# Second FFN, up projection, rounds 4 to 10: every unit as seven block products, with the weight sums made early in DRAM

## The reference, cut to what matters

```python
h = rms_norm_2(x, ffn_norm_g[l]) * (1 + scale_f) + shift_f
u, v = jnp.split(h @ w_up[l], 2, axis=-1)
u = causal_depthwise_conv(u, conv_w[l], conv_b[l])      # 3 taps along the tokens
x = x + gate_f * ((jax.nn.silu(u) * v) @ w_down[l])
```

## Time and profile before

| | us |
|---|---|
| median of 3 runs | 1345.59 (1345.52 to 1347.8) |
| the profiled execution | 1345.38 |
| its span, first to last instruction | 1343.4 |
| PE busy | 1331.0 |
| rounds 3 to 9, first block product to the first plain tile behind them (1043.77 to 1191.38) | 147.6 |

### The profile page before, as it was taken

The page is one execution under the profiler, slowest core; times in us unless marked ns, Lnnn a source line. Parts: engine busy times, 40 slices in busy tenths (PEclk is TensorE's granted clock), DMA queues, the critical chain, the costliest instruction groups (busy, mean ns, idle before and its releaser), DMA issues.

```text
span 1343.4 us, 21993 instructions
## 1 busy us (share of the span) xinstructions
PE 1331.0 (99%) x8268; PEld 1135.0 (84%) x8268; DVE 857.3 (64%) x1682; ACT 624.0 (46%) x1097; POOL 658.7 (49%) x369
## 2 busy tenths in 40 slices
PE   8999999999999999999999999999999999999998
PEld 7878888888998888888889976788998999988887
DVE  5898876456778676767897879724579454431222
ACT  7236566564364445453222525675344454542222
POOL 7555232126254444445553489733364776654441
PEclk9999999999999999999999999999999999999999
DMA  7931121115525444444673241121242223252221
GB/s 218 227 102 41 56 63 49 30 35 172 173 87 180 141 142 147 152 149 141 202 228 107 77 112 48 50 64 48 79 157 94 93 96 115 75 201 97 86 87 63
DMA packets 188903, 150.59 MB, mean 112 GB/s; under 512 B 21625, under 2 KB 186723, under 8 KB 188304
## 3 DMA queue, kind: packets, MB, share of 16 engines
q1 hardware_dynamic: 187104, 148.78, 35.8%
q10 hardware_dynamic: 1200, 0.36, 0.1%
q0 software_dynamic: 512, 0.25, 0.1%
HBM read 145.18 MB, written 4.19 MB: 111 GB/s over the span
## 4 chain that ended last, share of the span: by engine, by line
PE 93%; DVE 4%; ACT 1%; issue 1%; POOL 0%; DMA 0%; DVEq 0%; ACTq 0%
PE ps L2638 28%; PE ps L2639 27%; PE ps L2640 27%; PE ps L2832 2%; PE ps L2888 1%; PE ps L2917 1%; DVE qd L2291 1%; DVE hf L2299 1%; PE ps L3120 1%; PE ps L3164 0%; PE ps L3149 0%; PE ps L2722 0%; PE ps L3093 0%; PE ps L3186 0%; DVE hs L2334 0%
## 5 line engine op out<-in xcount | busy, mean ns | idle before, releaser
L914 POOL TENSOR_TENSOR w_lo<-raw,w_hi 128x1024 fp32r<-128x1024 f32 (+2 forms) x210 | 487.2, 2324 | 569.2 <-ACT w_hi L1021 436.0
L2638 PE MATMUL ps<-h_hi,w_hi 128*128 128x512 f32 (+1 forms) x1308 | 478.4, 366 | 0.1
L2639 PE MATMUL ps<-h_lo,w_hi 128*128 128x512 f32 (+1 forms) x1308 | 474.1, 362 | 0.0
L2640 PE MATMUL ps<-h_hi,w_lo 128*128 128x512 f32 (+1 forms) x1308 | 473.5, 362 | 0.0
L2638 PEld LDWEIGHTS ps<-h_hi,w_hi 128*128 128x128 f32 x1308 | 247.2, 189 | 41.9 <-issue 5.0
L2640 PEld LDWEIGHTS ps<-h_hi,w_lo 128*128 128x128 f32 x1308 | 247.1, 189 | 38.7
L1021 ACT ACTIVATE w_hi<-raw 128x1024 fp32r<-128x1024 f32 (+2 forms) x166 | 164.7, 995 | 244.4 <-PE ps L2640 222.9
L2639 PEld LDWEIGHTS ps<-h_lo,w_hi 128*128 128x128 f32 x1308 | 247.4, 189 | 35.6
L2638 PE MATMUL ps<-g_hi,w_hi 128*128 128x512 f32 (+1 forms) x394 | 144.9, 368 | 0.0
L2640 PE MATMUL ps<-g_hi,w_lo 128*128 128x512 f32 (+1 forms) x394 | 144.4, 366 | 0.0
L2639 PE MATMUL ps<-g_lo,w_hi 128*128 128x512 f32 (+1 forms) x394 | 144.3, 366 | 0.0
(11 more groups left out here) (408 smaller groups left out, 1999.2 us busy)
## 6 DMA issues: line engine op xcount, KB each, us to landing
ada<-in_ada_w SPq DMA_DIRECT2D x48, 512.0 KB, 3.7
raw<-in_ffn_w_up SPq DMA_DIRECT2D x22, 1024.0 KB, 4.9
raw<-in_w_up SPq DMA_DIRECT2D x22, 1024.0 KB, 4.9
raw<-in_w_in SPq DMA_DIRECT2D x21, 1024.0 KB, 5.1
raw<-in_ffn_w_down SPq DMA_DIRECT2D x8, 896.0 KB, 5.9
raw<-in_w_down SPq DMA_DIRECT2D x8, 896.0 KB, 5.0
raw<-in_w_in SPq DMA_DIRECT2D x16, 256.0 KB, 3.7
raw<-in_w_out SPq DMA_DIRECT2D x4, 1024.0 KB, 5.1
```

Source lines behind the costliest of these rows:

```text
L914: pool.tensor_tensor(w_lo[slot % 4][:, 0:nk, :], part[:, :, slot % 2 * P:(slot % 2 + 1) * P], w_hi[slot % 4][:, 0:nk, :].bitcast(F32), ALU ...
L2638: pe.matmul(out_ap, w, x, start=first, stop=False, **kw)
L2639: pe.matmul(out_ap, w, xl, start=False, stop=False, **kw)
L2640: return pe.matmul(out_ap, wl, x, start=False, stop=last, **kw)
```

## The change

What was done for u is done for v as well: rounds 3 to 9 consist of 14 pairs of tiles (`NPAIR`), each made of seven products, and no plain tile is left in them. The order of the products on PE is the list `PRODUCTS`: of pair p the products 6 and 2, the next pair's 1, then 7 and 3, the next pair's 5, then 4. Each product has half a weight buffer (`half_slot`), so that ACT may begin a product's high part when PE has ended the product eight places before. The pairs use PSUM banks 4 to 7 and 0 to 3 in turn.

The four sums of weight blocks are no longer made by DVE in each round. They are made once, for all seven rounds, in DRAM (`kept_sums`, four tensors of 2 x 512 x 7 x 128): POOL issues 8 DMAs that copy a block (`begin_sum`, one behind the low part of each of the tiles 20 to 27) and 8 DMAs that add another block or an earlier sum (`add_to_sum`, behind tiles 30, 31, 32, 33, 34, 36, 38, 40). A DMA moves 512 x 7 x 128 floats. The first 12 have pieces of 128 floats, the last four, which add one sum to another, pieces of 896. POOL waits for landings at three places: for the 8 copies ahead of the first addition, for the first four additions ahead of the fifth (behind tile 34), for six ahead of the seventh (behind tile 38). SP then loads, for each pair, three blocks early and the rest late (`early_blocks`, `late_blocks`): six DMAs in place of one, 1792 KB in place of 1024 KB.

The low parts are split between two engines: products 2, 3 and 4 have theirs made by DVE (`DVE_LOWS`), products 1, 5, 6 and 7 by POOL. The sums are formed with the other sign in part, so that the second tile of a pair comes out negative; its taps and the product with v are multiplied by -1 at no extra instruction but one on DVE ahead of the FFN. The space that DMA descriptors of POOL take in SBUF is halved (8192 bytes a partition), and the 8192 bytes hold the loaded sums (`sums`).

```diff
 R0, R1 = 3, FT // 2 - 1
-IN_ORDER = (1, 5, 6, 2, 7, 3, 4)
+PAIR_TILE, AFTER = S_UP2 + 4 * R0, S_UP2 + 4 * R1
+NPAIR = (AFTER - PAIR_TILE) // 2
+
+
+PRODUCTS = [(0, 1), (0, 5)]
+for _p in range(NPAIR):
+    PRODUCTS += [(_p, 6), (_p, 2)] + [(_p + 1, 1)] * (_p + 1 < NPAIR) + [(_p, 7), (_p, 3)] \
+        + [(_p + 1, 5)] * (_p + 1 < NPAIR) + [(_p, 4)]
+PRODUCT = {x: q for q, x in enumerate(PRODUCTS)}
+NQ = len(PRODUCTS)
+DVE_LOWS = (2, 3, 4)
...
+def product_lows(p, j):
+
+    mine = [x for x in PRODUCTS[:PRODUCT[p, j] + 1] if (x[1] in DVE_LOWS) == (j in DVE_LOWS)]
+    return len(mine) if j in DVE_LOWS else PAIR_TILE + len(mine)
+
+
+def w_slot(s):
+    return s % 4 if s < AFTER else (PAIR_TILE + NQ // 2 + s - AFTER) % 4
+
+
+def half_slot(p, j):
+    q = PRODUCT[p, j]
+    return (PAIR_TILE + q // 2) % 4, slice(q % 2 * 4, q % 2 * 4 + 4)
 
...
+        def early_blocks(p):
+
+            c = up_columns(R0 + p // 2, p % 2)
+            return [(w_of(p, 1), k_tiles(a["w_up_2"][0], 0, 4, c, P)), (w_of(p, 5), kept_sum(1, p)), (w_of(p, 6), kept_sum(2, p))]
+
+        def late_blocks(p):
+
+            c = up_columns(R0 + p // 2, p % 2)
+            view = raw[(PAIR_TILE // 2 + p) % 2][:, :].rearrange("p (k n) -> p k n", k=KD)
+            return [(view[:, 4:8, :], k_tiles(a["w_up_2"][0], 4 * P, 4, c)), (w_of(p, 7), kept_sum(3, p)), (w_of(p, 3), kept_sum(4, p))]
+
+        def kept_blocks(kind, t, kh):
+
+            c = up_columns(R0, kind)
+            w = a["w_up_2"][0][kh * 4 * P:(kh + 1) * 4 * P, c:c + (R1 - R0) * 256]
+            return w.rearrange("k (r t n) -> k r t n", t=2, n=P)[:, :, t, :]
```

SP, POOL (the line numbers in the changed kernel are 983 for `begin_sum`, 993 for `add_to_sum`):

```diff
+            sp.wait_ge(sums_kept, SUMS_BEGUN + 16 * 8)
+            sp.wait_ge(freed["dve"], FREED[up_tile(0, 1, 1)][1])
+            for p in range(NPAIR):
+                n = PAIR_TILE // 2 + p
+                if p < 2:
+                    after_lows(2 * n - 3)
+                else:
+                    sp.wait_ge(lo_done, product_lows(p - 2, 6))
+                for dst, src in LOADS[n]:
+                    sp.dma_start(dst, src).then_inc(raw_in[n % 2], 16)
+                if p >= 2:
+                    after_lows(2 * n - 3)
+                for dst, src in late_blocks(p):
+                    sp.dma_start(dst, src).then_inc(late_in[n % 2], 16)
+            for n in range(AFTER // 2, S_DOWN2 // 2 + 2):
                 unit(n)
...
+            def begin_sum(n, kind):
+
+                t, kh = {1: (1, 0), 2: (0, 0), 3: (0, 0), 4: (0, 1)}[n]
+                pool.dma_start(kept_sums[n - 1][kind], kept_blocks(kind, t, kh)).then_inc(sums_kept, 16)
+
+            def add_to_sum(n, kind):
+
+                if n == 1:
+                    pool.wait_ge(sums_kept, SUMS_BEGUN)
+                elif n in (2, 4):
+                    pool.wait_ge(sums_kept, SUMS_BEGUN + 16 * (4 if n == 2 else 6))
+                more = {1: lambda: kept_blocks(kind, 1, 1), 2: lambda: kept_sums[0][kind],
+                        3: lambda: kept_blocks(kind, 1, 0), 4: lambda: kept_sums[1][kind]}[n]()
+                pool.dma_start(kept_sums[n - 1][kind], more, accum_op=ALU.add, max_dma_last_dim=4 * (R1 - R0) * P).then_inc(sums_kept, 16)
+
+            SUM_STEPS = dict(zip(range(S_MERGE + 2, S_MERGE + 10), itertools.product((1, 2, 3, 4), range(2))))
+            ADD_STEPS = dict(zip([S_MERGE + 12, S_MERGE + 13, S_MERGE + 14, S_MERGE + 15] + [S_ATTN + 2 * n for n in range(4)],
+                                 itertools.product((1, 3, 2, 4), range(2))))
 
             def tables():
```

ACT and DVE (in the changed kernel 2535 is `product_low`, 2607 `seed_c12`, 2611 `make_c22`):

```diff
+            def product_hi(q):
+
+                if q >= NQ:
+                    return
+                p, j = PRODUCTS[q]
+                u = PAIR_TILE // 2 + p
+                if q < 8:
+                    act.wait_ge(tile_done, PAIR_TILE - 3 + q // 2)
...
                     act.wait_ge(raw_in[u % 2], RAW_COUNT[u])
                 else:
-                    act.wait_ge(w_summed, ONCE + 4 * (r - R0) + {5: 1, 7: 2, 6: 3, 3: 4}[j])
-                act.activation(w_hi[w][:, ks, :], w_of(r, j), ACT.Copy).then_inc(hi_done, 1)
+                    act.wait_ge(late_in[u % 2], LANDED + 48 * (p // 2 + 1))
...
+            for p in range(NPAIR):
+                r, kind = R0 + p // 2, p % 2
+                last = R0 + (p - 1) // 2
+                q0 = PRODUCT[p, 6] + 7
+                if p and not kind:
+                    g_high(last, 0)
+                if kind:
+                    first_tap(last, 1)
+                if p == NPAIR - 1:
+                    hi(AFTER)
+                product_hi(q0)
+                if kind:
+                    silu(last, 0)
+                product_hi(q0 + 1)
+                if p == NPAIR - 1:
+                    hi(AFTER + 1)
+                if kind:
+                    silu(last, 1)
+                elif p:
+                    g_high(last, 1)
+                product_hi(q0 + 2)
+                if p + 1 < NPAIR:
+                    copy_one(p + 1)
+                    product_hi(q0 + 3)
...
+                if p + 1 < NPAIR:
+                    product_hi(q0 + 5)
+                    copy_five(p + 1)
+                    product_hi(q0 + 6)
+            hi(AFTER + 2)
...
+            def product_low(p, j):
+                w, ks = half_slot(p, j)
+                dve.wait_ge(hi_done, product_splits(p, j))
+                dve.tensor_tensor(w_lo[w][:, ks, :], w_of(p, j), w_hi[w][:, ks, :].bitcast(F32), ALU.subtract).then_inc(low_by_dve, 1)
+
...
+            for p in range(NPAIR):
+                r, kind = R0 + p // 2, p % 2
+                last = R0 + (p - 1) // 2
+                if kind:
+                    taps2(last, 1)
+                elif p:
+                    gated_up(last, 1)
+                product_low(p, 4)
+                seed_c12(p)
+                if p + 1 < NPAIR:
+                    product_low(p + 1, 2)
+                if p and not kind:
+                    g_low(last, 0)
+                if not kind:
+                    g_low(last, 1)
+                make_c22(p)
+                if p + 1 < NPAIR:
+                    product_low(p + 1, 3)
+                if kind:
+                    gated_up(r, 0)
+                else:
+                    taps2(r, 0)
```

PE:

```diff
-                pe.wait_ge(lo_done, SPLIT_NO[r, j])
+                if j in DVE_LOWS:
+                    pe.wait_ge(low_by_dve, ONCE + product_lows(p, j))
+                else:
+                    pe.wait_ge(lo_done, product_lows(p, j))
                 if j == 1:
-                    pe.wait_ge(freed["dve"], FREED[up_tile(r - 1, 0, 0)][1])
+                    pe.wait_ge(freed["dve"], FREED[PAIR_TILE + 2 * (p - 2) if p > 1 else PAIR_TILE - 4][1])
...
                 elif j == 7:
-                    pe.wait_ge(c12_seeded, ONCE + r - R0 + 1)
+                    pe.wait_ge(c12_seeded, ONCE + p + 1)
                 elif j == 4:
-                    pe.wait_ge(c22_made, ONCE + r - R0 + 1)
+                    pe.wait_ge(c22_made, ONCE + p + 1)
...
-            for r in range(R0, R1):
-                s = up_tile(r, 1, 0)
-                product(r, 1)
...
+            for p, j in PRODUCTS:
+                product(p, j)
+            pe.wait_ge(freed["dve"], after_pair(NPAIR - 2))
+            for s in range(AFTER, S_DOWN2):
                 tile(s, h_hi, h_lo)
```

349 lines of the change are left out of this document (150 added, 199 removed).

## The result

The changed kernel took 1375.2 us in the median of four runs (1370.9 to 1376.7), the kernel before 1346.7 beside it: ratio 1.020, 95% interval 1.017 to 1.024. Forecast were 1339.7 us. The profiled execution took 1376.2 us (span 1374.1), 30.8 more than that of before.

The account below looks back on a forecast made before the run. PE was taken as the bound. From the profiled 1345.38 us, 5.9 came off in the block rounds and all else cost 0: 1339.5, with the median 0.2 above, 1339.7; 8 in 10 range 1338 to 1355.

Parts of the forecast that it names:

- PE's gain: Block rounds 3 to 9: seven rounds of matmuls fall from 147.0 to 141.1 us, 5.9 us gained; stage forecast 141.7.
- Engines beside PE: Block rounds, per pair of 10.08 us: ACT 7.3, POOL 5.6, DVE 6.5 to 9.5; none becomes the bound.
- The tightest hand-off: Pairs of v in the block rounds: product 7 waits for `seed_c12`, ready at 4.0 us, wanted by PE at 4.3.
- It just fits: Pairs of v: the seed is ready before PE wants it, with 0.1 to 0.3 us to spare.
- DVE ends at 3.6: Pairs of v: DVE's low part, begun at 2.5 beside POOL's, ends 3.6 us after product 4 of the pair before.
- The rival of a late seed: Block rounds: seed at 4.9, PE stands 0.5 to 0.8 us a pair, 4 to 9 us, 1345 in all; chance 0.15.
- POOL's time for a DMA: Merge gates: issuing a DMA of 3584 pieces holds POOL 2 to 3 us; up to 6.6 us costs nothing.
- Landing of an addition: Sums in DRAM, from 218.5 us: an addition takes 16 us to land, between 10 and 30.
- Cost 0: Sums in DRAM: additions land before tiles 35 and 39 need POOL's low parts, so they cost nothing, with thin cover.
- Additions land late: Rival: POOL waits for landings behind tiles 34 and 38, about 20 us slower, 1360; decides from 17.6 us; chance 0.20.
- Loads: Block rounds: 1792 KB a pair at DMA share 0.6 to 0.7, hidden; DRAM sums: eight DMAs fit beside the loads.
- Slow descriptors: Rival: POOL needs 15.9 us to issue each DMA in the merge gates, about 1420 us in all; chance 0.10.

Follow-up runs that it names:

- with the seed in time, the one without additions, low part first: Changed kernel without its eight additions, DVE's low part of product 4 put ahead of the taps in each pair: 1343.4 us, ratio 0.9963.
- the last kernel above: Changed kernel with product 4's low part first, copies behind tiles 21 to 24 and 34 to 37, additions behind 27, 29, 31, 33, 144, 146, 148, 149: 1343.3 us.
- the spread kernel with copies from tile 18: Changed kernel with copies behind tiles 18 to 25, additions behind 27, 29, 31, 33, 144, 146, 148, 149, product 4's low part first: 1350.6 us.

## Why the prediction was wrong, step by step

**PE's gain: right.** 5.9 us were forecast; with the seed in time the rounds took 141.40 us against a forecast of 141.7, 6.2 less than before. In the changed kernel they took 143.8, a gain of 3.8; the 2.4 missing are the one wait in the last pair.

**Engines beside PE: right, somewhat high.** In the rounds DVE was busy 84.9 / 14 = 6.1 us a pair (forecast 6.5 to 9.5), ACT 6.5 (7.3), POOL 5.7 (5.6), the DMA share 0.55 (0.6 to 0.7).

**The tightest hand-off: right for 13 pairs, missed in the last.** "It just fits" held where I counted, a middle pair. I had not counted the edge, where POOL's operation is a plain low part of 128x1024 (2.41 us, back to back with a second) and not one of 128x512. What did not hold there is "DVE ends at 3.6" beside POOL's low part: here DVE's took 2.47 us, 1.8 more than the 0.68 it takes alone, and ended 0.5 us behind the first of POOL's two (1214.24 + 2.4 is 1216.6; DVE ended at 1217.2). The rival of a late seed is thus true in one pair of 14.

**POOL's time for a DMA: right.** A copy of 3584 pieces held POOL 2.2 to 2.4 us (2 to 3 taken), an addition 3.6 (1.0 where it reads sums), all under the 6.6 that were free. But that limit spoke only of PE's lead over POOL in the merge gates. It did not speak of what stands behind the issue for another engine, such as low parts of the queries. Nor did it speak of DVE: while POOL issues a DMA, and again while it makes a low part, `sc` of DVE stands. With a copy alone beside it, issued at 283.61 for 2.34 us in the last kernel above, two multiplications took 2.62 us in place of 1.00:

```profile
284.04 2.62 DVE L2087 TENSOR_SCALAR sc<-sc,stat,gates 128x512 f32<-128x512 f32 x2
```

I had that hold in the block rounds, between two low parts, and put it at nothing in the merge gates, where DVE is what PE waits for in the 1.3 us of the changed kernel and in most of the 9 with the copies two tiles earlier.

**Landing of an addition: the size right, the overlap wrong. This is the step that failed.** I took 16 us; the median of all eight is 16.7 (12.9 to 20.2), and the four that read `w_up_2` took 16.4 to 18.8. "With 16 us, overlapping in part, this holds" took two in flight at once. Up to the seventh none were: POOL stood until the one before had landed, 65 us in all. The first four took from 220.84 to 292.38, 17.9 us each against my own limit of 17.6 from 218.5. The fifth and the sixth followed one after the other and landed at 319.29, where I had them by 300. So "Cost 0" was 17.6 us at tile 39.

**Its rival: right in kind, too small.** "Additions land late" had 0.20 and 20 us, with POOL behind tiles 34 and 38 the place, and 17.6 us the point from which it decides. For what it counted it was near: 17.6 us by tile 39. At tile 35 nothing waited in the end: its low part was there by 296.3 us at the latest, and PE, late by then through its waits for DVE, began the tile at 305.04. The price was 29 us because the rival left out two things. An addition makes other loads late: 15.1 us for 512 KB in place of 3.3, which is 9.0 us more by the convolution branch. And PE that had stood was granted half its clock behind it, 2.4 us there. The runs with the additions in the first down projection show the late loads by themselves: POOL had time there, and the loss was larger, not smaller.

**Loads: right for copies, put at nothing for additions without a reason.** I had "Eight in 72 us fit beside the loads, which leave the engines mostly idle there", of copies. For additions there is no such sum; the rival names the loads of 512 KB, without a price. For copies that is right (0.3 us in the median). An addition holds the engines far longer for the same bytes. Worked out from the share of the software queue: in the spread kernel with copies from tile 18, 0.753 x 80 us / 4 = 15.1 us of all engines for an addition from `w_up_2`, 0.563 x 70 / 4 = 9.9 us for one from sum to sum, against 0.481 x 85 / 8 = 5.1 for a copy. The share adds up the times of packets and can pass 1.00 (1.01 and 1.06 above), so these are estimates of what an addition takes, and best read against one another.

```profile
q0 software_dynamic: 14390, 7.34, 75.3%
...
q0 software_dynamic: 2112, 7.34, 56.3%
...
q0 software_dynamic: 3712, 14.68, 48.1%
```

The three rows are the software queue's packets, MB and share from 195 to 275 and 870 to 940 us of that spread kernel and from 120 to 205 us of the one without additions, low part first. The Trainium skill, Collectives: The Full Stack, § The bandwidth ceiling, has an add at half the rate of a copy. From sum to sum that is what the trace shows (9.9 against 5.1); for the additions from `w_up_2` it is a third (15.1). There the rows hold 14390 packets for four additions, some 3600 each, where eight copies have 3712, 464 each. That the small packets are the reason is likely, and no run here separated it.

**Slow descriptors: did not come** (0.10).

The chances stood at 0.24 for slower. The forecast rested on a cover that I had called thin; the limit of 17.6 us against a landing taken as 16 with ends at 10 and 30 would have borne far more than 0.20 for that rival, and its own 1360 already lay outside the range of 8 in 10.

## What to carry to other kernels

Before a DMA is put on an engine's queue as "hidden", ask three things of its place: how long until the next one may be issued (the engine stands, with all that is queued behind), which loads land in the same stretch, and who else waits for what stands behind the issue or, like DVE here, stands itself while it is made. Spread to stretches with few loads, with the additions from `w_up_2` 20 us apart and nothing due behind a landing, sixteen such transfers cost 1.4 us here (1343.3 against 1341.9, intervals that overlap); bunched, they cost 30 (1375.2 against 1344.9).

For two engines that cannot run the same form side by side, count the hand-off at the edges of a stage too, where the neighbour's operation is another size, and put the one that PE waits for first.

## What the hardware showed that I had not expected

- An adding DMA from DRAM to DRAM held the DMA engines 15.1 us for 1.8 MB in 512-byte pieces and 9.9 in 3584-byte ones, a copy 5.1, by the times of its packets.
- While POOL issued a DMA of 3584 pieces, a DVE operation between SBUF operands stood: two of 128x512 took 2.62 us beside the issue of a copy (2.34 us), and 5.16 beside that of an addition with a low part queued behind it, in place of 1.00.
- With additions of 512-byte pieces the next DMA was not issued before the one before had landed; of copies the second was (125.64 and 132.99 us in the kernel without additions, 10.3 and 12.7 us to landing), and the third, the fifth and the seventh stood 5.2, 4.3 and 3.5 us, until the one before had landed. From sum to sum it went both ways: in the changed kernel the sixth addition stood 9.96 us until the fifth had landed, with no wait in the program for that, and the eighth did not stand; in the recurrence the last two, 9.9 us apart, did not either. The likeliest reason is room for descriptors in the queue of POOL; no run here changed it.
- Loads of 512 KB took 15.1 and 19.3 us to land beside an addition, 3.3 without; beside plain copies of the same bytes 4.8 in the median.
- Behind waits of 2.3, 2.7, 5.4 and 7.0 us PE's clock was granted at half for a while, behind one of 3.2 us it was not. The four together cost some 8 us of PE's time beside 20.7 of waiting.
